# Second attention: v of all heads by seven block products in a stage of its own, through DRAM, and z pair by pair

## What is computed

```python
h = rms_norm(x, norm_g)
q, k, v, z = jnp.split(h @ w_in, 4, axis=-1)          # each 512 x 2048
q, k = rms_norm per 64 columns
weights = softmax(q0 k0 + bias) - lam * softmax(q1 k1 + bias)   # causal, per head
o = weights @ v                                        # 128 columns of v per head
o = rms_norm(o) * (1 - lam_0) * silu(z)
out = x + o @ w_out
```

## Time and profile before

| | us |
|---|---|
| median of 3 runs | 1262.78 |
| the runs | 1262.66 to 1268.88 |
| the profiled execution, its own time | 1263.26 |
| its span | 1261.5 |
| PE busy | 1252.8 |
| DVE busy | 868.6 |
| ACT busy | 628.9 |
| POOL busy | 284.4 |
| from the first scores of heads 2, 3 to those of 4, 5 | 58.7 |

### The profile page before, as it was taken

One profiled execution on the slowest core, in us unless ns is written; L12 is line 12 of the kernel. 1 busy time (PEld: TensorE's weight loads), 2 busy tenths in 40 slices (PEclk: granted clock), 3 DMA queues, 4 the chain that ended last, 5 costly groups with the idle time before them and its releaser, 6 DMA issues.

```text
span 1261.5 us, 18580 instructions
## 1 busy us (share of the span) xinstructions
PE 1252.8 (99%) x7226; PEld 1072.6 (85%) x7226; DVE 868.6 (69%) x1642; ACT 628.9 (50%) x1284; POOL 284.4 (23%) x188
## 2 busy tenths in 40 slices
PE   9999999999999999999999999999999999999999
PEld 7788888889889999999888888888888888888887
DVE  5435665677479889888954647676767677677753
ACT  4436655444444444444644445556555555556530
POOL 2022310000046666660002412021212112020000
PEclk9999999999999999999999999999999999999999
DMA  7322232323441442333246222222223332223611
GB/s 238 110 59 76 59 100 68 101 87 112 155 182 56 146 134 87 115 118 100 68 150 233 101 68 79 90 84 85 93 85 98 104 93 84 85 84 118 243 60 67
DMA packets 106410, 134.82 MB, mean 107 GB/s; under 512 B 9681, under 2 KB 73425, under 8 KB 106322
## 3 DMA queue, kind: packets, MB, share of 16 engines
q1 hardware_dynamic: 96146, 112.39, 27.7%
q10 hardware_dynamic: 10176, 21.24, 4.7%
HBM read 123.91 MB, written 9.70 MB: 106 GB/s over the span
## 4 chain that ended last, share of the span: by engine, by line
PE 94%; DVE 4%; issue 1%; ACT 1%; POOL 0%; DMA 0%; ACTq 0%; DVEq 0%
PE ps L1184 13%; PE ps L1186 13%; PE ps L1185 13%; PE ps L1189 8%; PE ps L1191 7%; PE ps L1190 7%; PE ps L1456 5%; PE ps L1459 5%; PE ps L1458 5%; PE ps L1559 3%; PE ps L1569 1%; PE ps L1541 1%; DVE wlo L2023 1%; PE ps L1519 1%; PE ps L1518 1%; PE ps L1517 1%
## 5 line engine op out<-in xcount | busy, mean ns | idle before, releaser
L2023 DVE TENSOR_TENSOR wlo<-raw,whi 128x512 fp32r<-128x512 f32 (+1 forms) x290 | 248.0, 880 | 107.9 <-ACT whi L1622 107.0
L1622 ACT ACTIVATE whi<-raw 128x512 fp32r<-128x512 f32 (+2 forms) x334 | 218.8, 686 | 94.2 <-PE ps L1186 35.6
L1184 PE MATMUL ps<-whi,hth 128*128 128x512 f32 x464 | 189.2, 408 | 0.0
L1186 PE MATMUL ps<-wlo,hth 128*128 128x512 f32 x464 | 181.4, 391 | 0.0
L1185 PE MATMUL ps<-whi,htl 128*128 128x512 f32 x464 | 181.2, 391 | 0.0
L2593 POOL TENSOR_TENSOR wlo<-raw,whi 128x384 fp32r<-128x384 f32 (+1 forms) x44 | 49.1, 1133 | 410.4 <-ACT whi L1622 410.4
L1189 PE MATMUL ps<-hth,whi 128*128 128x512 f32 (+1 forms) x352 | 139.5, 396 | 0.0
L1191 PE MATMUL ps<-hth,wlo 128*128 128x512 f32 (+1 forms) x352 | 134.1, 381 | 0.0
L1190 PE MATMUL ps<-htl,whi 128*128 128x512 f32 (+1 forms) x352 | 134.0, 381 | 0.0
L1184 PEld LDWEIGHTS ps<-whi,hth 128*128 128x128 f32 x464 | 87.4, 188 | 20.6 <-issue 3.1
L1186 PEld LDWEIGHTS ps<-wlo,hth 128*128 128x128 f32 x464 | 87.1, 188 | 19.3
(11 more groups left out here) (424 smaller groups left out, 3114.0 us busy)
## 6 DMA issues: line engine op xcount, KB each, us to landing
raw<-in_w_gate_up SPq DMA_DIRECT2D x44, 512.0 KB, 4.8
raw<-in_l_w_in SPq DMA_DIRECT2D x32, 512.0 KB, 4.4
raw<-in_l_w_in SPq DMA_DIRECT2D x16, 1024.0 KB, 5.3
raw<-in_w_in SPq DMA_DIRECT2D x13, 1024.0 KB, 5.2
raw<-in_w_down SPq DMA_DIRECT2D x10, 1024.0 KB, 4.9
raw<-in_l_w_out SPq DMA_DIRECT2D x8, 1024.0 KB, 5.0
raw<-in_w_in SPq DMA_DIRECT2D x26, 256.0 KB, 3.3
raw<-in_w_branch SPq DMA_DIRECT2D x8, 512.0 KB, 4.1
```

What stands on the lines that cost most here:

```text
L1184: e.matmul(o, ah, wh[:, cs], start=a, stop=False, skip_group_check=skip)
L1186: m = e.matmul(o, ah, wl[:, cs], start=False, stop=z, skip_group_check=skip)
L1622: return e.activation(out, in_, ACT.Copy, **how)
L2023: return e.tensor_tensor(out, src, hi_part.bitcast(F32), ALU.subtract)
```

## The change

- `proj2(0)` ends with q and k. The new `values()` follows: z of pair 0 (`pz`, 48 matmuls), and then v of all heads. v is 512 x 1024 (tokens by depth) times 1024 x 2048; for each half u of the columns the operands are cut in 2 x 2 blocks, and seven block products `vp u p` (24 matmuls each) replace eight. Four sums of activations (`vf`, eight DVE operations of 128x1024, L2679), their high and low parts (`vh`), four differences of weights (`vt`, L2698), the high and low part of each block (`vb`), kept partial results (`v1`, `v5`, `vu`, `vk`, ACT) and sums of results (`vc`, DVE) go with them. The results go to DRAM (`vs`).
- In the pairs, `proj2(g)` has q, k and z of pair g alone: 96 and 48 matmuls. Pair g's v is loaded from DRAM behind a load of a later pair's weights and split by `vv` (ACT, and DVE 128x1024) in the middle of `pair(2g)`.
- `merge` spreads the 14 pieces over 20 slots. z's slots are twice as long as q's and k's.
- Scores wait for the key blocks that they use instead of all four. Seven semaphores for constants become one.

```diff
@@ Weights
-        for g in range(8):
-            for k in (0, 4):
-                self.add(4, 512, [(256 * i, 4, 0, kview(w_in2, k, 4, E2 * i + 256 * g, 256)) for i in range(2)])
-            for k in (0, 4):
-                self.add(4, 512, [(0, 4, 0, kview(w_in2, k, 4, E2 * (2 + g % 2) + 512 * (g // 2), 512))])
+        zw = lambda g: self.add(8, 256, [(0, 8, 0, kview(w_in2, 0, 8, 3 * E2 + 256 * g, 256))])
+        self.qk[0] = [qk(0, k) for k in (0, 4)]
+        for g in range(UP):
+            self.z[g] = zw(g)
+        for u in range(2):
+            for k, c in ((0, 0), (0, 512), (4, 512), (4, 0)):
+                self.h[self.add(4, 512, [(0, 4, 0, kview(w_in2, k, 4, 2 * E2 + 1024 * u + c, 512))])].pre = []
+        for g in range(1, 8):
+            self.qk[g] = [qk(g, k) for k in (0, 4)]
+            if g >= UP:
+                self.z[g] = zw(g)
@@ Order.whole
+        self.values()
         for g in range(7):
-            merge(self.proj2(g + 1), 32, self.pair(2 * g), 14)
+            merge(self.proj2(g + 1), 16 if g + 1 < UP else 20, self.pair(2 * g), 14)
@@ Order.values
+        self.finish(z[2])
+        put("zg", 0, 0)
+        put("qt", *self.waiting.pop(0), self.bank())
+        put("vf", 2)
+        put("vh", 0)
+        self.value_sum(0, 0)
+        self.finish(z[3])
+        put("zg", 0, 1)
+        for i in range(3, 8):
+            put("vf", i)
+        self.value_split(0, 1)
+        for u in range(2):
+            product(u, 0)
+            each("v1", u)
+            self.value_sum(u, 1)
+            self.value_split(u, 2)
+            if u == 0:
+                put("vh", 1)
+            product(u, 1)
...
@@ Order.pair
         put("t2", even, 0, bank())
+        put("vv", even // 2)
@@ PE, s2
-                    pe.wait_ge(qk2_lo, 8 * g + 8)
+                    pe.wait_ge(qk2_lo, 8 * g + (4, 6, 8)[ev])
@@ PE, p2
-                    pe.wait_ge(v2_lo, 8 * (g // 2) + 8)
+                    pe.wait_ge(v2_lo, g + 1)
@@ SP, after load(n)
+                for g in range(8):
+                    if n == (W.qk[g + 1][1] if g == 0 else W.z[min(g + 1, 7)] + (g == 7)):
+                        for i in range(4):
+                            sp.wait_ge(v_out[i], 32 * (g // 4 + 1))
+                        if g < 3:
+                            sp.wait_ge(mm, V_DONE)
+                        else:
+                            sp.wait_ge(p2_pe, 2 * (g - 3) + 2)
+                        e.dma_start(v2l_f[g % 3][:, :, :], v_block(g)).then_inc(v_in[g % 3], 16)
```

More of the change, by code:

```diff
@@ L52 @@
 GATED = 2
+UP = 1
 class Once:
@@ L207, in __init__ @@
         self.gate_parts = self.count("gh", "bs")
-        self.block_behind = [self.mm[o if isinstance(o, tuple) else W.h[o].last] for o in self.block_behind]
+        self.block_behind = {b: self.mm[o if isinstance(o, tuple) else W.h[o].last] for b, o in self.block_behind.items()}
         self.hi, self.lo = {}, {}
@@ L510, in block_split, with value_split, value_sum, value_product @@
             self.put("us", p, c)
+    def value_split(self, u, p):
+        self.block_slot[u, p] = len(self.owners) % 2
+        self.block_behind[u, p] = self.owners[-2]
+        self.owners.append(("vp", u, p, 1, 2))
+        for c in range(2):
+            self.put("vb", u, p, c)
+    def value_sum(self, u, q):
+        for c in range(2):
+            self.put("vt", u, q, c)
+    def value_product(self, u, p):
+        for t in range(2):
+            for i0 in (0, 2):
+                self.put("vp", u, p, t, i0)
@@ new lines, in each, with values @@
+    def each(self, *step):
+        for t in range(2):
+            self.put(*step, t)
+    def values(self):
+        put, each, product = self.put, self.each, self.value_product
+        z = [self.gate2(g, i, m) for g in range(UP) for i in range(2) for m in range(2)]
+        self.finish(z[0])
+        put("qs", 0, 3)
+        put("vf", 0)
+        self.finish(z[1])
+        put("qt", *self.waiting.pop(0), self.bank())
+        put("vf", 1)
+        self.value_split(0, 0)
+        self.finish(z[2])
+        put("zg", 0, 0)
+        put("qt", *self.waiting.pop(0), self.bank())
+        put("vf", 2)
[14 more added lines that the diff above has]
+            product(u, 1)
+            each("v5", u)
+            self.value_split(u, 3)
+            if u == 0:
+                put("vh", 3)
+            self.value_sum(u, 2)
+            product(u, 2)
+            each("vu", u)
+            self.value_split(u, 4)
+            if u == 0:
+                put("vh", 2)
+            product(u, 3)
+            each("vc", u, 0)
+            self.value_split(u, 5)
+            product(u, 4)
+            each("vs", u, 0)
+            each("vc", u, 1)
+            self.value_sum(u, 3)
+            self.value_split(u, 6)
+            product(u, 5)
+            each("vs", u, 1)
+            each("vc", u, 2)
+            if u == 0:
+                self.value_split(1, 0)
+                self.value_sum(1, 0)
+            else:
+                self.split(self.W.qk[1][0], 4)
+            product(u, 6)
+            each("vs", u, 2)
+            each("vk", u)
+            each("vs", u, 3)
+            if u == 0:
+                self.value_split(1, 1)
@@ L656, in proj2 @@
         for i, tb in order:
-            u = self.unit(n + i, 16, 4, "pj", g, 0, i, tb)
+            u = self.unit(self.W.qk[g][i], 16, 4, "pj", g, i, tb)
             next(u)
             yield
+            if g == 2 == UP and i == 0 and tb < 2:
+                self.put("qt", *self.waiting.pop(0), self.bank())
+                if tb == 0:
+                    self.put("qs", 1, 3)
             if (i, tb) == (1, 1):
@@ L670, in proj2 @@
             yield
-        tail = 0
-        for i in range(2):
-            for tb in range(TB):
-                yield from self.unit(n + 2 + i, 16, 4, "pj", g, 1, i, tb)
-                if tail == 0:
-                    self.put("qs", g, TB - 1)
-                elif tail < 3:
-                    self.put("qt", *self.waiting.pop(0), self.bank())
-                tail += 1
-                if i == 1:
-                    self.put(("vs", "zg")[g % 2], g, tb)
-                yield
+        if g < UP:
+            return
+        for i, m in ((0, 0), (0, 1), (1, 0), (1, 1)):
+            u = self.gate2(g, i, m)
+            next(u)
+            if (i, m) == (0, 0):
+                self.put("qs", g, TB - 1)
+            self.finish(u)
+            if (i, m) in ((0, 1), (1, 0)):
+                self.put("qt", *self.waiting.pop(0), self.bank())
+            if i == 1:
+                self.put("zg", g, m)
+            yield
     def scores(self, h, ev):
@@ L780, in last_heads @@
         put("t2", 14, 0, bank())
+        put("vv", 7)
         put("xb", (2,))
@@ L1035, in build @@
         ut_d = sem("ut_d")
+        v_out = [sem(f"v_out_{n}") for n in ("c12", "c22", "c11", "c21")]
+        v_in = [sem(f"v_in{i}") for i in range(3)]
         gf_d, g_hi, g_lo, g_d, g_a = (sem(n) for n in ("gf_d", "g_hi", "g_lo", "g_d", "g_a"))
@@ L1955, in _ @@
                         act.wait_ge(oz_d, h - 4)
-                    e.activation(zg[h % 5][:], ps[PJ[tb]][:, :], ACT.Tanh, scale=0.5).then_inc(z_a, 1)
+                    e.activation(zg[h % 5][:], ps[PJ[m2 + (2 if g == 1 and UP == 2 else 0)]][:, :], ACT.Tanh,
+                                 scale=0.5).then_inc(z_a, 1)
                 elif kind == "s2":
```

321 lines of the change are left out of this document (243 added, 78 removed).

## The result

The changed kernel took 1325.05 us (median of 4 runs, 1321.46 to 1330.86) against 1265.83 us of the kernel before on the same chip (median of 4 runs, 1262.66 to 1269.42: the three of the table and one more). The ratio is 1.047, with a 95% interval of 1.043 to 1.051. The forecast was 1284 us with a range of 1268 to 1298: right in sign, 41 us short in size. The profiled execution took 1328.53 us, 1326.8 of them its span.

What follows compares the result with a forecast made beforehand. TensorE, busy for 1252.8 of 1261.5 us, was taken to bound the kernel. 1261.5 - 10.9 + 9.9 + 21.2 = 1281.7, with 1 for a slow restart a span of 1282.7, gave 1284 us; range 1268 to 1298.

Steps and rivals of the forecast that it cites:

- The matmuls removed: Computing v of all heads: 48 matmuls of 512 columns go, at 0.227 us each, worth 10.9 us.
- The start of the v stage: TensorE stands for DVE's queue, 8.4 us ahead of product 1 and 1.4 ahead of product 2; sum +9.9 us.
- The bank waits: Merged pairs: TensorE waits for qkl to free block 1's bank, 3.3 us a pair, 1.4 in the first; 21.2 us.
- The pairs as a whole: From first scores to the next pair's: some 51 us, 58.66 before, with a rest ahead of scores released by qkl.
- a rival at 0.10: DVE falls further behind: qn late by 1.5 us in each pair and the last pair blocked, 1297; chance 0.10.
- The clock in the pairs: A pause ahead of the scores, then matmuls at 1.2 GHz; up to 3 us in each of seven pairs, 1305; chance 0.05.
- The last pair and ScalarE's block: Last pair: ScalarE waits for half of z's matmuls before overwriting their operand; up to 4 us, in the range only.
- Loads and v's return: Weight loads and v's way out and back come in time, priced at nothing; rival of late v: 1290, chance 0.03.

Runs made afterwards that it cites:

- the kernel with even slots and a light DVE: Changed kernel with 24 even slots, projection banks, v's low part late, and most of DVE's q, k, z weight low parts left out in pairs 2 to 7; 1283.8 us.

## Why the prediction was right or wrong, point by point

- **The matmuls removed**: right, as far as the runs come near it. A pair with no waits would be 47.8 us; the kernel with even slots and a light DVE came to 49.5, 1.2 of it rests.
- **The start of the v stage**: right, sized by its own steps. The rest ahead of product 1 was forecast at 8.4, released by DVE's low part. Here is the row of the changed kernel:

```profile
756.79 0.77 PE L1703 MATMUL ps<-whi,v2h 128*128 128x512 f32 x1 [8.95 <-DVE wlo L2230]
```

  With the start that the earlier 5.9 us give it, product 1 came 0.8 us later than forecast. The clock was low until 761.2: the first ten matmuls took 4.4 us instead of 2.3, a loss of 2.1 where 1 was taken; the wait of 1.4 ahead of product 2 did not come, because the slow product gave DVE the time. The second half had no wait. The cause, DVE's queue, is shown by the run with z of two pairs ahead.
- **The bank waits**: right. The rests that qkl releases came to 21.1 us in the seven pairs, where 21.2 was forecast. They are two in each pair and not one: 1.9 to 2.5 us for the bank of block 1, inside the bounds of 1.4 to 4.4, and 0.95 for the bank of block 0, for which "I put nothing for them" stood. That bank was used again after some 4.4 us of TensorE work, more than the 2.0 to 2.4 that the working had looked at, but its qkl stands in the same late part of DVE's queue. The chain that was counted, from the transpose's start to the end of qkl of block 1, took 4.7 us instead of 4.4 (968.49 to 973.17), and the rest for block 0 lies inside it. So the sum fits for a reason; that it fits to 0.1 us is luck.
- **The pairs as a whole**: the step that failed is that the sum has 3.3 us a pair (21.2) for the bank wait and nothing beside it. The pairs lost 58.3 us. First, qn itself: the working says that "now it is later still in its queue", behind v's 1.14 us, then gives this to a rival at 0.10 as 1.5 a pair and puts it at nothing in the sum. It was 1.7 to 2.1 us in every pair, 14.1 in all. Second, the clock, put at nothing: 14 us. What remains is 1.9 us of waits that only the last pair has, and the 7 us that come with the rests. The rests are 37.1 us in all.
- **The clock in the pairs** had a chance of 0.05 and was the case: it fell in all seven pairs, for 6.8 or 10.2 us each. The rival's "up to 3 us in each of seven pairs" was the right size (the filled rests give 14 us in all, 2 a pair), its chance was not. The reason given against it, that no pause in the trace shows it, was none: the kernel before has no pauses there, and the forecast itself put one of 3.3 us into each pair. The rule quoted beside it from the Trainium skill, "TensorE: Matmul & The Clock Gate", section "Part 1: The HAM clock gate", that idleness lets the clock drop and sustained work releases it, agrees with these traces: 1.00 all through the pairs whose rests were filled, 0.50 from the first or second rest on in every pair of the changed kernel, and 1.00 again with TensorE back at work.
- **The last pair and ScalarE's block**: nothing in the sum, up to 4 in the range. This pair lost 11.6 us against 7 to 9 of the others; the rests of 1.20 ahead of the head product (for ptl) and 0.65 ahead of the last stage's first unit (for zg) are its own. That ScalarE's block makes them was not shown: with that block moved, the rest ahead of the head product stayed (1.44) and a longer one came at the last stage.
- **Loads and v's return**: priced at nothing, and TensorE waits for neither. In the v stage of the changed kernel ScalarE waited twice for a load of weights (6.9 us, the longest 3.6) and DVE twice (1.9), with no rest of TensorE behind them. No engine waited for v's return.
- **The chances**: the two rivals that lay above the forecast were priced as alternatives to it (0.10 and 0.05), where they are links of one chain with it: bunched steps make rests, rests lower the clock. Joined, 1297 and 21 more, they give 1318; measured were 1321 to 1331.

## What to carry to other kernels

Work taken off the engine that sets the end is worth its time only if the others' answers move up with it: here DVE's 41.5 and ScalarE's 33 us of steps in a pair had fitted behind 58.6 us of matmuls, and 38.6 and 31 did not fit behind 47.8: every late place in their queues showed. Where steps are handed out by a ratio, print how close a bank's or a block's last use and next use come, and add up the in-order queue of the engine that frees it. Do it for every reuse and every operand, not for the shortest alone, and keep each wait in the sum. And on a fully busy TensorE price a rest twice: itself, and what the clock does behind it.

## What the runs showed of the hardware that was not expected

- The granted clock fell around quite short rests. In the changed kernel it fell in every pair behind the first rest (1.7 to 2.1 us): in five pairs before the second one (0.95) had ended, in the other two 0.9 us behind it, in none behind the third. With rests of 0.3 to 0.75, 0.95 and 0.3 to 0.5 us within 5 us it fell in five pairs of one run and not in the two others. Rests of up to 1.4 us spread over a pair (3.1 to 4.7 us in all) did not lower it in pairs 1 to 5 of three runs.
- Once down in a pair, it stayed at 0.50 for 3.4, 6.8 or 10.2 us, in the changed kernel for half of that time or more with TensorE back at work. The pairs of one kernel differ in how long.
- More matmuls made the kernel faster: 21 idle ones in each pair for a gain of 14 us in the pairs.
- Matmuls of 256 columns started 0.113 us apart in one execution and 0.118 in another over 175 us, at the same granted clock; the two rows of each kernel are 45 matmuls apart. Before:

```profile
500.02 0.28 PE L1456 MATMUL ps<-sh,whi 128*128 128x256 f32 x1
...
505.12 0.28 PE L1456 MATMUL ps<-sh,whi 128*128 128x256 f32 x1
```

  After:

```profile
503.06 0.28 PE L1593 MATMUL ps<-sh,whi 128*128 128x256 f32 x1
...
508.36 0.28 PE L1593 MATMUL ps<-sh,whi 128*128 128x256 f32 x1
```

  What makes the difference stays open.
